# Two of an expert's six weight loads move from SyncE to ScalarE, behind the eviction that frees their slots

## The reference, cut to what matters

```python
h = (xb @ w1[e] + b1[e])                       # w1[e]: 1024 x 2048
h_glu = minimum(h[:, :1024], 7);  h_lin = clip(h[:, 1024:], -7, 7)
act = h_glu * sigmoid(1.702 * h_glu) * (h_lin + 1.0)
y = act @ w2[e] + b2[e]                        # w2[e]: 1024 x 1024
```

## Time and profile before

| | us |
|---|---|
| median of 3 runs (1090.41 to 1091.3) | 1091.23 |
| the profiled execution, its own time | 1092.27 |
| its span, from the first to the last instruction | 1090.3 |
| PE busy in the span | 983.2 |
| ScalarE busy in the span | 117.4 |

### The profile page before, as it was taken

The page is one execution under the profiler, slowest core; times in us unless marked ns, Lnnn a source line. Parts: engine busy times, 40 slices in busy tenths (PEclk is TensorE's granted clock), DMA queues, the critical chain, the costliest instruction groups (busy, mean ns, idle before and its releaser), DMA issues.

```text
span 1090.3 us, 13890 instructions
## 1 busy us (share of the span) xinstructions
PE 983.2 (90%) x5869; PEld 425.6 (39%) x5869; DVE 230.1 (21%) x531; ACT 117.4 (11%) x226; POOL 20.3 (2%) x24
## 2 busy tenths in 40 slices
PE   6997878999999999988889888998988888898885
PEld 4644544344444444433333333333333333333332
DVE  1577344111111111111111001111111111110113
ACT  1053130000000000000000000000000000000002
POOL 0010020000000000000000000000000000000000
PEclk9998998999999999999999999999999999999998
DMA  9924746999999999999999999999999999999993
GB/s 319 287 110 209 308 154 253 429 421 417 394 426 426 429 427 429 429 427 429 429 429 428 429 428 429 428 429 429 429 429 428 429 428 429 428 429 429 429 429 161
DMA packets 33093, 421.31 MB, mean 386 GB/s; under 512 B 4880, under 2 KB 5136, under 8 KB 7376
## 3 DMA queue, kind: packets, MB, share of 16 engines
q1 hardware_dynamic: 33072, 421.02, 92.6%
HBM read 419.95 MB, written 1.05 MB: 386 GB/s over the span
## 4 chain that ended last, share of the span: by engine, by line
PE 49%; DMA 42%; DVE 5%; ACT 2%; issue 1%; POOL 0%; SPq 0%; POOLq 0%; DVEq 0%
DMA ring<-in_w_dram 41%; PE bank L1354 20%; PE bank L1388 12%; PE bank L1057 4%; PE bank L1325 3%; PE bank L1318 3%; PE bank L1265 1%; PE bank L1370 1%; ACT work L573 1%; PE bank L1253 1%; PE bank L1274 1%; DMA h<-in_x_dram 1%; ACT work L522 1%; PE bank L1198 0%; PE bank L1143 0%
## 5 line engine op out<-in xcount | busy, mean ns | idle before, releaser
L1354 PE MATMUL bank<-ring,work 128*64 128x512 f32 x2016 | 458.0, 598 | 51.2 <-DMA ring<-in_w_dram 50.0
L1354 PEld LDWEIGHTS bank<-ring,work 128*64 128x64 f32 x2016 | 166.6, 136 | 324.2 <-issue 210.7
L1388 PE MATMUL bank<-ring,work 128*64 128x512 f32 x1024 | 226.8, 595 | 15.5 <-ACT work L573 15.5
L975 DVE TENSOR_SCALAR work<-bank 128x512 f32<-128x512 f32 x32 | 22.1, 692 | 726.9 <-PE bank L1354 726.9
L1388 PEld LDWEIGHTS bank<-ring,work 128*64 128x64 f32 x1024 | 71.2, 137 | 150.5 <-issue 132.9
L570 ACT ACTIVATE work<-work 128x512 f32<-128x512 f32 x32 | 20.2, 632 | 539.1 <-DVE work L975 539.1
L1325 PE MATMUL bank<-work 64*128 64x512 f32 x256 | 63.6, 615 | 0.7 <-ACT work L581 0.7
L1318 PE MATMUL bank<-work,tok 128*128 128x64 bf16 x1056 | 50.8, 194 | 0.0
L1318 PE MATMUL bank<-work 128*128 128x64 bf16 x528 | 49.0, 195 | 1.2 <-DVE work L948 1.2
L1318 PEld LDWEIGHTS bank<-work,tok 128*128 128x128 bf16 x1056 | 47.4, 99 | 0.0
L1318 PEld LDWEIGHTS bank<-work 128*128 128x128 bf16 x528 | 33.7, 99 | 27.2 <-issue 27.2
(11 more groups left out here) (190 smaller groups left out, 487.8 us busy)
## 6 DMA issues: line engine op xcount, KB each, us to landing
ring<-in_w_dram SPq DMA_DIRECT2D x190, 2048.0 KB, 33.1
ring<-in_w_in_dram SPq DMA_DIRECT2D x8, 1168.0 KB, 18.7
work<-in_w_dram SPq DMA_DIRECT2D x2, 2048.0 KB, 12.0
ring<-in_w_out_dram SPq DMA_DIRECT2D x2, 1024.0 KB, 14.5
ring<-in_w_out_dram SPq DMA_DIRECT2D x1, 2048.0 KB, 21.1
h<-in_x_dram SPq DMA_DIRECT2D x2, 512.0 KB, 4.7
out_dram<-tok SPq DMA_DIRECT2D x4, 256.0 KB, 2.4
tok<-in_b_dram SPq DMA_DIRECT2D x3, 256.0 KB, 16.6
```

What stands on the lines that cost most here:

```text
L975: nc.vector.tensor_scalar(glu, bank[2][:, :], LIMIT, None, ALU.min).then_inc(S.glu_ready, 1)
L1354: last = mm(bank[(2, 5)[g]][j * CAP:(j + 1) * CAP, :], xg[:, k * CAP:(k + 1) * CAP], chunk[:, r, g * FF + j * FG:g * FF + (j + 1) * FG], s ...
L1388: last = mm(bank[6][j * CAP:(j + 1) * CAP, :], hidT[:, r, s * CAP:(s + 1) * CAP], chunk[:, r, j * 512:(j + 1) * 512], start=s == 0 and r == 0,
```

## The change

From chunk 0 of expert 5 on, chunks 0 and 1 of each expert are loaded by ScalarE. The function `load_ahead` issues both directly behind the eviction of the expert two before, without a wait of its own: the eviction's wait for `chunk_used` covers both slots. SyncE skips these two chunks and issues chunks 2 to 5 as before. The slots, the semaphores of the slots, and PE's waits are the same. ScalarE's last four experts are written out behind its loop, so that the last two experts of the last round load nothing ahead; in between, with more rounds, expert numbers wrap at 32.

```diff
+BY_ACT = 2
+AHEAD = 2
...
+        def w1_chunk(e, r):
+            return w1[e].rearrange("(c p r) n -> c p (r n)", p=P, r=W1_ROWS)[r]
...
-                    sp.dma_start(to, w1[e].rearrange("(c p r) n -> c p (r n)", p=P, r=W1_ROWS)[r]).then_inc(loaded, 16)
+                    sp.dma_start(to, w1_chunk(e, r)).then_inc(loaded, 16)
...
                 for used in range(start, start + PER_BODY):
-                    refill(it, used, (it * UNROLL + (SLOTS + used) // PER_EXPERT) % EXPERTS)
+                    if (SLOTS + used) % PER_EXPERT >= BY_ACT:
+                        refill(it, used, (it * UNROLL + (SLOTS + used) // PER_EXPERT) % EXPERTS)
             last = rounds * bodies + whole
             for used in range(start, (bodies - whole) * PER_BODY - SLOTS):
-                refill(last, used, whole * UNROLL + (SLOTS + used) // PER_EXPERT)
+                if (SLOTS + used) % PER_EXPERT >= BY_ACT:
+                    refill(last, used, whole * UNROLL + (SLOTS + used) // PER_EXPERT)
...
+            def load_ahead(n, q):
+
+                for r in range(BY_ACT):
+                    s = slot_of((q + AHEAD) * PER_EXPERT + r)
+                    act.dma_start(slot(s), w1_chunk((n + AHEAD) % EXPERTS, r)).then_inc(slot_in[s], 16)
+
             for n in range(UNROLL):
                 expert(n)
+            load_ahead(UNROLL - 1, UNROLL - 1)
             bodies = EXPERTS // UNROLL
             act.wait_ge(S.extra_done, 1)
             rounds = act.value_load(extra[0:1, 0:1], min_val=0, max_val=ROUNDS - 1)
-            with act.Fori(1, rounds * bodies + bodies) as it:
+            with act.Fori(1, rounds * bodies + (bodies - 1)) as it:
                 for q in range(UNROLL):
                     expert(it * UNROLL + q)
+                    load_ahead(it * UNROLL + q, q)
+            final = rounds * EXPERTS + (EXPERTS - UNROLL)
+            for q in range(UNROLL):
+                expert(final + q)
+                if q + AHEAD < UNROLL:
+                    load_ahead(EXPERTS - UNROLL + q, q)
```

More of the change, by code:

```diff
@@ L581, in expert @@
                 nc.scalar.activation(res, bank[6][:, :], ACT.Copy).then_inc(S.res_ready, 1)
+            def load_ahead(n, q):
+                for r in range(BY_ACT):
+                    s = slot_of((q + AHEAD) * PER_EXPERT + r)
+                    act.dma_start(slot(s), w1_chunk((n + AHEAD) % EXPERTS, r)).then_inc(slot_in[s], 16)
+            assert SLOTS == AHEAD * PER_EXPERT - (PER_EXPERT - BY_ACT) and (UNROLL - 1 + AHEAD) * PER_EXPERT >= PEELED
+            assert (UNROLL - 2 + AHEAD) * PER_EXPERT + BY_ACT <= PEELED
             for n in range(UNROLL):
                 expert(n)
+            load_ahead(UNROLL - 1, UNROLL - 1)
             bodies = EXPERTS // UNROLL
```

## The result

The changed kernel takes 1104.09 us in the median of four runs (1098.49 to 1106.96), the one before 1091.17 (1090.41 to 1091.3) beside it: a ratio of 1.0103, 95% interval 1.0075 to 1.0131. In a second measurement of the same kernel, with more runs of both, it is 1099.91 (1098.32 to 1104.35, 6 runs) against 1091.94 (1090.17 to 1095.86, 29 runs): 1.0069, 1.0047 to 1.009. Slower, by 8 to 13 us; in the first measurement it also scatters more. The profiled execution took 1104.5 us, with a span of 1102.1, 11.8 more than the 1090.3 of before.

The account below looks back on a forecast made before the run. Transfers were taken to pace the experts, with engines 1.01 busy at 428 GB/s. Late issue 3.9 plus end order 4.4 gave +8.3 us: 1099.5 for the median, own range 1098 to 1102, stated range 1091.5 to 1106.

Parts of the forecast that it names:

- Later issue: At expert 5 the pair's loads go out at 278.4 instead of 274.54, onto a dry queue: +3.9 us, once.
- the case for which 3.3 was given: At expert 5, ScalarE's sequencer issues the pair while the eviction runs: 3.3 us without a ring load instead of 3.9.
- Issues off SyncE, and two loads on ScalarE: 54 loads of about 0.35 us leave mostly waiting SyncE, no gain; on ScalarE 14 us cover 0.7 us of issues, no cost.
- Equal shares: In steady experts both queues take turns packet by packet; the pair needs 19.6 us, is through by about 22, period unchanged.
- some 9: Steady expert: chunk 3 of the next expert lands some 9 us after the eviction; PE would take it at 10.5.
- order kept: Rival: the two queues' loads land in order of issue, so only the +3.9 stays, 1095.1 us; chance 0.16.
- a starved pair: Rival: SyncE's backlog goes first, expert 31's pair lands last, +19.5, 1110.7 us; chance 0.13 together with disturbed streams.
- more bandwidth: Rival: a second list fills gaps from 280 to 1060 us; 1.6% more repays 8.3 us; chance 0.18.
- The wait moves to chunk 5, and the end: PE's 3.2 us wait moves to each expert's sixth chunk; last evictions 26.1 apart, +4.4 us of work at the end.

Follow-up runs that it names:

- the control without loads: Changed kernel's program, ScalarE's last four experts written out, but SyncE issues all loads: 1091.76 us against 1092.01 for the kernel before, ratio 0.9998.
- the one with 48 loads in the middle: Changed kernel, but ScalarE loads only for experts 6 to 29, SyncE for expert 5 and the last two: 1091.2 us, ratio 0.9993 to the kernel before.
- first at once: Changed kernel, but ScalarE issues chunk 0 once chunk 4 of the expert two before is used, chunk 1 behind the eviction: 1095.81 us, 1.0032.
- chunk 1 only: Changed kernel, but ScalarE loads only chunk 1 of each expert from the sixth on, SyncE chunk 0 as before: 1095.67 us, ratio 1.003.

## Why the prediction was right, and where it was not

The forecast was 1099.5, of its own range 1098 to 1102. The first median, 1104.09, lies above that, the second, 1099.91, on the forecast. That the second came so near is in part luck: the sum had 0.7 us too much for the late issue and nothing for the clock.

*Later issue.* Right in kind and place: once, at expert 5, and never again. Its size was 3.2 us, not 3.9. ScalarE's sequencer issued at 282.70 while the eviction of 282.69 ran, the case for which 3.3 was given.

*Issues off SyncE, and two loads on ScalarE.* Nothing either way, as forecast; the control without loads and the one with 48 loads in the middle both show it.

*Equal shares.* The pair issued at 309.0 and 309.5 lands after 14.1 and 24.2 us, 10.1 apart; alone on all engines a chunk takes 4.9, so it had about half of them:

```profile
DMA to landing us min/median/max: 14.1/14.1/14.1
...
DMA to landing us min/median/max: 24.2/24.2/24.2
```

The first of the pair took 14.1 us, and not the 9.8 of half shares. For some 4 us it got little: behind the pair issued at 1036.24, the next chunk of SyncE's queue landed 5.5 us after the last one (1041.18), and only the one behind it took 9.8 us (1050.99). Why is open. It mattered in one place: by half shares from the start, chunk 3 of the next expert would land 11.6 us behind the eviction, not at the prediction's "some 9", and PE would have waited there about 1 us; it landed after 8.5 (1013.66 behind the eviction at 1005.16), and L1376 waits nowhere. That figure of the prediction does not follow from its own rule and came out right. The rivals of order kept and of a starved pair fall with this, and more bandwidth falls with the 428 GB/s.

*The wait moves to chunk 5, and the end.* Right: L1410 waits, L1376 doesn't; PE starts chunk 5 of expert 30 at 1060.20, as it lands, and 1079.7 - 4 x 4.89 is 1060.1; evictions of 30 and 31 are 26.10 apart, and the term is 4.4 as it was worked out.

*What was left out* is the clock. I moved a wait from 2 x 1.2 us to about 3 us in one piece and counted it as the same idle time. The granted clock stayed at 1.00 through the short waits; around waits of 3 us it fell to half (from the 2.4 GHz level to 1.2), at nine of the 14 waits of 2.9 us or more in the first profile and at ten of 14 in the second. Such a fall makes the chunk longer and the next expert's wait shorter (1.3 to 1.7 us, or none), and behind that shorter wait the clock held each time. In the middle transfers cover all that. At expert 30 they don't, and there it depends on where the falls before it lay: in the first profile the clock had fallen at expert 29, so expert 30 waited 1.36 us and kept it; in the second it had not, the wait was 3.06 us, and the fall cost 2.9 us. That may be part of why runs of the changed kernel lie above the sum of 7.6 us; two profiles can't show how often it happens. It was no term of the sum and should have been one of 0 to 2.9.

The other 4.9 us of the first profile are in the attention part, before the first changed instruction has run, with a stretch at half clock there. The second profile of the same kernel doesn't have them, and runs of the kernel before, beside the experiments, reach 1095.86 and 1097.96. E3 lies anywhere from 275.8 to 282.7 in the ten profiles. The three latest (282.7, 280.8 in first at once, 279.8 in chunk 1 only) are of kernels in which ScalarE loads, but four other profiles of such kernels have 275.8 to 276.8; the three of kernels without its loads have 276.7 to 277.8. First at once has a stretch at half clock near 60 us too (0.86 and 0.80 in the same windows), chunk 1 only has none. What makes an execution lose this time is open, and so is whether the change makes it more frequent; the first measurement's 12.9 us are the larger for it, as far as its one profile shows.

## What to carry to other kernels

A second issuing queue gives no bandwidth when the engines are full, but it changes the order of landing: its loads soon took about half of the engines here and overtook those that were needed first. Before loads are split over queues, count for each awaited chunk how many places it lands ahead of the last one and how much work stands behind it; check every chunk that is overtaken, not just the last. And where transfers pace the kernel, look at its ends: a late issue costs where the queue is dry, and a wait moved into the last stages costs where nothing behind it can hide it. Two short waits are not the same as one long wait of their sum: the long one can cost TensorE's clock.

## What the runs showed of the hardware that I had not expected

ScalarE issues a load while its own activation runs: both started at 282.69 and 282.70. The first load behind a dry queue landed after 7.7 us. Two queues with loads of 2 MB each got about half of the engines, and together the 428 GB/s of one. Of the clock of TensorE: idle stretches of 1.2 to 1.7 us left it at 1.00; those of about 3 us brought 0.54 to 0.73 over the chunk behind them in 19 cases of 28 in the two profiles of the change; matmuls of no use in the wait, 1.91 us of them, kept it at 1.00 in every expert that had them.
